# Seven products of block sums for eight products of blocks in the up projection of an encoder layer's feed-forward part

## The reference

```python
def conv_ffn(xn, conv_prev, w_up, conv_w, conv_b, w_down):
    L = xn.shape[1]
    h = xn @ w_up
    hp = jnp.concatenate([conv_prev.astype(h.dtype), h], axis=1)
    hc = conv_b + sum(conv_w[j] * hp[:, j:j + L] for j in range(CONV_W))
    a, b = jnp.split(hc, 2, axis=-1)
    return (jax.nn.gelu(a) * b) @ w_down, hp[:, L:]
```

## Time and profile before

| | us |
|---|---|
| median of 3 runs | 1023.45 (1022.51 to 1023.83) |
| the profiled execution, its time | 1022.95 |
| its span | 1021.2 |
| PE busy in the span | 998.8 |
| DVE, ACT, POOL busy | 543.6, 386.7, 86.2 |

### The profile page before, as it was taken

How to read it: one execution, slowest core, us unless ns; L and a number is a source line. 1 busy time by engine, 2 the same in 40 slices (tenths; PEclk the granted TensorE clock), 3 DMA queues, 4 the chain that set the end, 5 groups by cost and what they waited for, 6 DMA issues and landing times.

```text
span 1021.2 us, 17140 instructions
## 1 busy us (share of the span) xinstructions
PE 998.8 (98%) x6814; PEld 942.8 (92%) x6814; DVE 543.6 (53%) x838; ACT 386.7 (38%) x667; POOL 86.2 (8%) x247
## 2 busy tenths in 40 slices
PE   4999999999999999999999999999999999999997
PEld 4999999888999999999997899999999999888886
DVE  5238978754322266614454768666666666312214
ACT  5343435766322246421224645333333333312212
POOL 4100000000022101002000001000000001000000
PEclk9999999999999999999999999999999999999999
DMA  7612121111232125438346433232233232312323
GB/s 244 139 57 76 49 83 42 42 42 43 89 105 65 54 99 176 141 109 269 108 152 234 134 125 89 83 84 83 83 83 85 82 88 84 107 62 83 92 103 114
DMA packets 103956, 104.25 MB, mean 102 GB/s; under 512 B 13634, under 2 KB 88242, under 8 KB 103904
## 3 DMA queue, kind: packets, MB, share of 16 engines
q1 hardware_dynamic: 97600, 81.06, 26.7%
q0 software_dynamic: 6304, 22.47, 6.3%
HBM read 89.84 MB, written 13.67 MB: 101 GB/s over the span
## 4 chain that ended last, share of the span: by engine, by line
PE 94%; ACT 2%; DVE 1%; issue 1%; DMA 1%; SPq 0%; ACTq 0%; DVEq 0%
PE ps L1388 19%; PE ps L1390 19%; PE ps L1389 19%; PE ps L1397 7%; PE ps L1399 7%; PE ps L1398 7%; PE ps L1550 2%; PE ps L1528 2%; PE ps L1407 1%; PE ps L1408 1%; PE ps L1536 1%; PE ps L1512 1%; PE ps L1476 1%; PE ps L1591 1%; PE ps L1468 1%
## 5 line engine op out<-in xcount | busy, mean ns | idle before, releaser
L1388 PE MATMUL ps<-xs,whi 128*128 128x288 f32 x1312 | 391.8, 299 | 0.2 <-issue 0.2
L1390 PE MATMUL ps<-xs,wlo 128*128 128x288 f32 x1312 | 386.6, 295 | 0.0
L1389 PE MATMUL ps<-xs,whi 128*128 128x288 f32 x1312 | 386.3, 294 | 0.0
L1388 PEld LDWEIGHTS ps<-xs,whi 128*128 128x128 f32 x1312 | 246.2, 188 | 1.7 <-issue 0.8
L1389 PEld LDWEIGHTS ps<-xs,whi 128*128 128x128 f32 x1312 | 246.2, 188 | 0.7 <-issue 0.2
L1390 PEld LDWEIGHTS ps<-xs,wlo 128*128 128x128 f32 x1312 | 246.1, 188 | 0.0
L1040 DVE TENSOR_TENSOR wlo<-raw,whi 128x2048 fp32r<-128x2048 f32 (+2 forms) x45 | 99.5, 2212 | 143.4 <-ACT whi L715 143.3
L715 ACT ACTIVATE whi<-raw 128x2048 fp32r<-128x2048 f32 (+2 forms) x47 | 86.2, 1833 | 100.4 <-PE ps L1399 88.0
L1397 PE MATMUL ps<-whi,xs 128*128 128x256 f32 (+2 forms) x264 | 86.1, 326 | 0.0
L1399 PE MATMUL ps<-wlo,xs 128*128 128x256 f32 (+2 forms) x264 | 83.3, 316 | 0.0
L1398 PE MATMUL ps<-whi,xs 128*128 128x256 f32 (+2 forms) x264 | 83.3, 316 | 0.0
(11 more groups left out here) (269 smaller groups left out, 1518.2 us busy)
## 6 DMA issues: line engine op xcount, KB each, us to landing
raw<-in_w_up SPq DMA_DIRECT2D x44, 512.0 KB, 5.0
raw<-in_w_in SPq DMA_DIRECT2D x21, 1024.0 KB, 5.6
raw<-in_w_down SPq DMA_DIRECT2D x10, 1024.0 KB, 5.1
raw<-in_w_out SPq DMA_DIRECT2D x6, 1024.0 KB, 5.1
gate_scratch<-stage POOLq DMA_DIRECT2D x16, 288.0 KB, 2.6
gates_in<-gate_scratch POOLq DMA_DIRECT2D x8, 576.0 KB, 4.3
raw<-in_w_branch_gla SPq DMA_DIRECT2D x4, 1024.0 KB, 5.1
silu_scratch<-stage POOLq DMA_DIRECT2D x8, 288.0 KB, 4.8
```

The costliest lines, as they stand in the source:

```text
L1388: pe.matmul(out, wh[:, k, c0:c0 + P], xh[:, k, t], start=(k == 0), stop=False)
L1389: pe.matmul(out, wh[:, k, c0:c0 + P], xl[:, k, t], start=False, stop=False)
L1390: ins = pe.matmul(out, wl[:, k, c0:c0 + P], xh[:, k, t], start=False, stop=(k == kn - 1))
```

## The change

From panel 2 on, the product of a panel is cut into two by two blocks: the two column halves (a, b), the two feature halves (1, 2) and the two token halves. The weight blocks are A1, A2, B1, B2 and sit in `raw` in the order B1, A1, A2, B2 (three DMAs per panel now, where there were two). POOL makes four sums of weight blocks, each 128x512, in `bsum`, which lies in the same memory as `wlo`: S1 = B1 + B2, S3 = A1 - B1, S2 = S1 - A1, S4 = A2 - S2. Four sums T1 to T4 of token blocks, each 128x1152, are made once by DVE from `x_all`, the unsplit tokens, which POOL gets by adding `xhi` and `xlo`. Seven products of 4 feature blocks (12 matmuls each, `product`) replace eight; each raises `prods`. ACT and DVE add products up while copying them out of `ps`. ACT and DVE split A1, A2, B2 (1536 columns, into `qhi` and `qlo`) and the four sums (twice 1024, into `whi` and `wlo`). The first tap moves from DVE to ACT, and u = ca * cb from DVE to POOL, which writes it unsplit to `u_all`; u is split group by group, in the last panel and during the down projection (`down_hi`, `down_lo`). Panels 0 and 1 keep their 96 matmuls.

The core of the diff, POOL first, then ACT, DVE and PE:

```diff
+            def whole_x(tt):
+                c = slice(tok(tt).start, tok(tt).start + rows(tt))
+                for kh in range(2):
+                    pool.wait_ge(x2lo_ready, 2 * tt + kh + 1)
+                    f = slice(4 * kh, 4 * kh + 4)
+                    nc.gpsimd.tensor_tensor(x_all[:, f, c], xhi[:, f, c].bitcast(F32), xlo[:, f, c].bitcast(F32), ALU.add)\
+                        .then_inc(x_all_ready, 1)
+            def block_sums(i, r):
+                j = 2 * i + r
+                ni, nr = following(i, r)
+                slot = up_slot(nr)
+                pool.wait_ge(raw_loaded[slot], up_loaded(ni, nr))
+                if isinstance(j, int) and j <= 2:
+                    pool.wait_ge(unit_done, UNITS2 + 2 * j)
+                reach(pool, prods, 7 * (j - 2))
...
+                nc.gpsimd.tensor_tensor(s1, b1, b2, ALU.add).then_inc(bsum_ready, 1)
+                nc.gpsimd.tensor_tensor(s3, a1, b1, ALU.subtract).then_inc(bsum_ready, 1)
+                pool.wait_ge(bsum_ready, 4 * j - 3)
+                nc.gpsimd.tensor_tensor(s2, s1, a1, ALU.subtract).then_inc(bsum_ready, 1)
+                pool.wait_ge(bsum_ready, 4 * j - 1)
+                nc.gpsimd.tensor_tensor(s4, a2, s2, ALU.subtract).then_inc(bsum_ready, 1)
+            def gated(i, r):
+                j = 2 * i + r
+                pool.wait_ge(gelu_ready, j + 1)
+                pool.wait_ge(ca_ready, 2 * j + 2)
+                nc.gpsimd.tensor_tensor(u_all[:, bass.ds(j, 1), :], ca[:, 0:UW].rearrange("p (o c) -> p o c", o=1),
+                                        cb[:, :].rearrange("p (o c) -> p o c", o=1), ALU.mult).then_inc(u_ready, 1)
+            def up_panel(i, r):
+                before = (i, 0) if r else (i - 1, 1)
+                block_sums(i, r)
+                tails(*before)
+                gated(*before)
+                rims(*following(i, r))
...
+            def up_panel(i, r):
+                first_sum(i, r)
+                gelu(*((i, 0) if r else (i - 1, 1)))
+                quad_split(i, r)
+                sum_split(i, r)
+                first_rows(i, r)
+                first_tap(i, r, 0)
+                first_tap(i, r, 1)
...
+            def up_panel(i, r):
+                u_sum(i, r)
+                v_sum(i, r)
+                quad_split(i, r)
+                rows_22(i, r)
+                sum_split(i, r)
+                rows_12(i, r)
+                rows_21(i, r)
+                conv(i, r, 0)
+                conv(i, r, 1)
...
+            def product(bank, wh, wl, xh, xl, opens):
+                out = ps[:, bank, 0:HALF]
+                for k in range(4):
+                    c = slice(P * k, P * k + P)
+                    pe.matmul(out, wh[:, c], xh[:, k, :], start=(opens and k == 0), stop=False, skip_group_check=True)
+                    pe.matmul(out, wh[:, c], xl[:, k, :], start=False, stop=False, skip_group_check=True)
+                    ins = pe.matmul(out, wl[:, c], xh[:, k, :], start=False, stop=(k == 3), skip_group_check=True)
+                ins.then_inc(prods, 1)
...
+                pe.wait_ge(lo_ready, UP0 + j + 1)
+                product(bank, *a1, *b11, True)
...
+                product(bank + 1, *s2, *t2, True)
...
+                product(bank + 2, *s1, *t1, True)
...
+                product(bank + 3, *s3, *t3, True)
+                pe.wait_ge(sum1_ready, j - 1)
+                product(bank, *a2, *b21, False)
+                pe.wait_ge(vsum_ready, j - 1)
+                product(bank + 2, *s4, *b22, False)
+                pe.wait_ge(c22_ready, j - 1)
+                product(bank + 3, *b2, *t4, False)
```

More of the change, by code:

```diff
@@ L1005, in _, with first_sum @@
-            with act.Fori(1, KF // 2 - 1) as i:
-                for r in range(2):
-                    up_rows(i, r)
-            for r in range(2):
-                up_rows(KF // 2 - 1, r, down=DOWN0 + r)
+            def first_sum(i, r):
+                j = 2 * i + r
+                act.wait_ge(prods, 7 * (j - 2) + 1)
+                act.wait_ge(ca_ready, 2 * j - 3)
+                act.wait_ge(tails_saved, 4 * j - 6)
+                nc.scalar.activation(ha[:, r, second], ps[:, 4 * (1 - r), 0:HALF], ACT.Copy).then_inc(sum1_ready, 1)
@@ new lines, in _ @@
+            first_tap(1, 0, 1)
+            up_panel(1, 1)
+            with act.Fori(2, KF // 2 - 1) as i:
+                for r in range(2):
+                    up_panel(i, r)
+            up_panel(KF // 2 - 1, 0)
+            first_sum(KF // 2 - 1, 1)
+            gelu(KF // 2 - 1, 0)
+            split(DOWN0)
+            act.wait_ge(prods, 7 * (KF - 3) + 4)
+            down_hi(0)
+            down_hi(1)
+            first_rows(KF // 2 - 1, 1)
+            split(DOWN0 + 1)
+            first_tap(KF // 2 - 1, 1, 0)
@@ L1010, in _ @@
+            first_tap(KF // 2 - 1, 1, 1)
+            gelu(KF // 2 - 1, 1)
             preload_sqrt()
@@ new lines, in _ @@
+            token_sums()
+            dve.wait_ge(pads_zero, 12)
+            for t in range(3):
+                token_lo(t)
+            quad_split(0, 1)
+            conv(0, 0, 0)
+            sum_split(0, 1)
+            conv(0, 0, 1)
+            u_sum(1, 0)
+            v_sum(1, 0)
+            token_lo(3)
+            quad_split(1, 0)
+            conv(0, 1, 0)
+            rows_22(1, 0)
+            conv(0, 1, 1)
+            sum_split(1, 0)
+            rows_12(1, 0)
+            rows_21(1, 0)
@@ new lines, in _ @@
+            conv(1, 0, 0)
+            conv(1, 0, 1)
+            up_panel(1, 1)
+            with dve.Fori(2, KF // 2 - 1) as i:
+                for r in range(2):
+                    up_panel(i, r)
+            up_panel(KF // 2 - 1, 0)
+            last = (KF // 2 - 1, 1)
+            u_sum(*last)
+            v_sum(*last)
+            split(DOWN0)
+            rows_22(*last)
+            down_lo(0)
+            rows_12(*last)
+            down_lo(1)
+            rows_21(*last)
+            split(DOWN0 + 1)
@@ L1675, in up @@
             def up(r, g, t):
-                return stationary_weights(ps[:, 4 * (1 - r) + 2 * g + t, 0:HALF], UP0 + r, KD, 256, P * g, xhi, xlo,
-                                          slice(HALF * t, HALF * t + HALF))
+                out = ps[:, 4 * (1 - r) + 2 * g + t, 0:HALF]
+                xt = slice(HALF * t, HALF * t + HALF)
+                slot = up_slot(r)
+                for k in range(KD):
+                    b = 4 + k if g == 0 else k if k < 4 else 8 + k
+                    wh, wl = whi[:, slot, P * b:P * b + P], wlo[:, slot, P * b:P * b + P]
+                    pe.matmul(out, wh, xhi[:, k, xt], start=(k == 0), stop=False)
+                    pe.matmul(out, wh, xlo[:, k, xt], start=False, stop=False)
+                    ins = pe.matmul(out, wl, xhi[:, k, xt], start=False, stop=(k == KD - 1))
+                return ins
             pe.wait_ge(x2lo_ready, 6)
```

371 lines of the change are left out of this document (274 added, 97 removed).

## The result

The changed kernel takes 1048.39 us (median of 4 runs, 1046.96 to 1049.45), the kernel before 1022.98 (4 runs beside it): 1.0246 times as long, 95% interval 1.023 to 1.0262. The profiled execution took 1046.96 us, with a span of 1045.2, 24.0 more than before.

The account below looks back on a forecast made before the run. PE bounded the kernel before; afterwards turns between DVE and POOL would bound the panel. Start +9 and +3, panels 3 to 20 +8.6, panel 21 -1.6: +19 us on 1022.95, 1042 us; range 996 to 1058.

Parts of the forecast that it names:

- the forecast's own case: Panels of 12.8 to 13.8 us, with 10.4 us of start and end: 1030 to 1058 us; chance 0.62.
- Removed from PE: Seven products per panel are 84 matmuls instead of 96, 11.13 us; over 20 panels 31.8 us less of PE.
- Turns: DVE instructions with two SBUF operands and POOL instructions reading SBUF take turns: together 12.8 to 13.8 us per panel.
- Panels 3 to 20: Steady part of the up projection's loop: 13.2 us per panel, 18 x 0.48 = +8.6 us.
- rival 2: A turn costs only the streaming of elements: panel 11.9 to 12.5 us, 1024 us, between 1015 and 1030; chance 0.12.
- turns alone suffice for a bound: Per panel, DVE's two-SBUF instructions (6.9 us) plus POOL's (5.9 to 6.9) bound the length, whoever has to wait.
- POOL's sum of 512 columns: One POOL block sum alone takes 1.08 to 1.26 us, priced from a row of 256 columns and one of 2.
- PE then waits at `lo_ready`, once per panel: In the loop the last `wlo` comes some 2 us after product 7, so PE waits there once per panel.
- The start: Before panel 2 PE starts late, at about 626.5, +9 us; panel 2 itself takes 15.7 us, +3.
- The end: The third group of u takes 17 us, hidden by 2 us behind the down projection's matmuls; put at 0.
- rival 1: No turns for large instructions: PE is the bound, panels of 11.13 us, 998 us; chance 0.20.

## Why the prediction was right

I predicted 1042 us, slower, with 0.70 on slower, a range of 1030 to 1058 for the forecast's own case and of 996 to 1058 over all; it is 1048.39, slower. The terms, against the span's 24.0:

- **Removed from PE**: right. The matmuls stand 0.13 apart as before, and with sums that only write the panel is 11.16 against the 11.13 of the text.
- **Turns**: right, and shown by the pair of runs with one more sum and one more write: reading costs, writing doesn't. By the Trainium skill, "SBUF — State Buffer", section "Who interferes with whom", a DVE instruction with two SBUF inputs contends with a GpSimd instruction that reads SBUF, not with one that only writes it; the shared ports are an exclusive lock, and issue order decides who blocks. The traces agree in both parts: taps at 0.82 beside writes of 0.53 and 0.96, and at 1.40 to 1.85 beside sums. That a DVE instruction waits behind a long POOL one, which the trace before didn't show, is in the rows of the panel above.
- **Panels 3 to 20**: 13.2 forecast, 13.39 measured; 18 x 0.67 = 12.1 instead of 8.6. The sum of turns itself came out: 12.8 to 13.8 forecast, and in the trace the turn is taken for 13.13 us and free for 0.26. A turn of a tap costs only the streaming (0.63), as rival 2 had it, but one of a sum 1.14 to 1.24 where rival 2 had 1.03, and its 11.9 to 12.5 did not come. The step that was loose is "turns alone suffice for a bound", with little lost beside them. That so little is lost is a property of this order of instructions: with u on DVE the turn is taken for 12.67 us, less than before, and the panel is longer. I had no term for DVE's round, which is what sets the length; that the full turn and DVE's round nearly coincide here is in part luck.
- **POOL's sum of 512 columns**: alone 1.28 (the least of L721 and L722), just over my upper end of 1.26. I took two ends from one row of 256 and one of 2.
- **"PE then waits at `lo_ready`, once per panel"**: wrong. It waits at three places (0.4 for `wlo`, 0.3 before product 6, 0.7 before product 7), since v and c22 are late in the same round of DVE; and the last `wlo` comes 0.4 us after product 7, where I had some 2. Each wait also makes the matmul behind it longer, 0.40 instead of 0.29, and the one after that starts 0.24 later instead of 0.13.
- **The start**: +12 forecast (9 and 3). Panel 2 starts at 626.13 against my 626.5, after 9.61 us of idle time, and panel 3 at 643.45 against 630.3: 13.2 in all. Panel 2 was mis-sized, 17.3 for 15.7. A part that I had not thought of is the clock: the granted clock is 0.50 and 0.51 in 620 to 630, that is 1.2 GHz, after PE had been idle from 616.5, and panel 2's first 16 matmuls take 3.87 us where 16 at 0.1325 take 2.1. Most of the rest is one wait: PE stands still for 3.3 us before panel 3, whose two `wlo` pieces, from 639.73, take 3.57 instead of 2.34, beside POOL's u of 2.26 from 639.96. The two pieces for panel 2, from 622.56, had taken 3.42 in the same way, and the three token splits 7.16 instead of the 4.1 that DVE alone would need.
- **The end**: right. Panel 21 is about 11.2 us and its taps are at 0.82; PE is busy for 20.00 of 20 us from 895 on, so the third group of u came in time.

13.2 + 12.1 - 1.5 is 23.8 of the 24.0 measured.

The run with writes in place of the sums, 1004.48, comes near rival 1 (no turns, 998): its panels are at that rival's 11.1, and what it takes beyond lies at the start, where PE still waits for 8.4 us and then twice runs at less than the full clock (granted 0.58 in 620 to 624 and 0.64 in 636 to 642). From there to the changed kernel it is 44 us, the price of four POOL sums per panel.

## What to carry to other kernels

When an engine gets work that was free by busy time, ask which of its operands come from where another engine reads too, and sum along the one engine that then has no pause: its own time, what holds it up there, its waits. Neither the busy shares nor the sum of both engines' exclusive time gives the length, and a wait taken away may come back as being held up. A trade that saves PE time and costs another engine needs only as much of it as that engine's slack can pay: every other panel gave 11.8 us, every panel cost 25. And look at the first round of a new loop apart; its late operands cost as much here (13.2 us) as eighteen panels of the steady state lose together (12.1).

## What the runs showed of the hardware

- A DVE instruction with two SBUF operands and a POOL instruction that reads SBUF go strictly in turn in the panels above, but one that has waited ends sooner after its turn comes than it takes alone: a tap of 0.82 ends 0.63 after the sum that blocked it, a sum of 1.28 ends 1.14 after the tap.
- A POOL copy of two columns takes 0.18, and 1.72 behind a `qlo` that began before it, so its length there tells of DVE's instruction in front.
- A POOL write of 1024 columns takes 0.96 us and one of 512 takes 0.53, less than half of a sum of 512 (1.28), and neither holds DVE up.
- While PE was idle for 9.61 us the granted clock fell to 0.50, and it was back at about 630, some 4 us after PE had started again. In the run with every other panel the clock stood at 0.50 from 638 to 642, after a wait of 6.0 us for panel 3; with 2.6 us of waits in all it stayed at 1.00.
- DVE makes a sum of 512 columns in 0.68 us, POOL in 1.28.
